# The first layer's start: modulation in pairs applied tile by tile, eight projections abreast, five modulation tiles later

## What is computed

```python
cond = silu(c)
for l in range(2):
    sh_a, sc_a, gt_a, sh_f, sc_f, gt_f = (cond @ w_ada[l] + b_ada[l]).reshape(6, 1024)
    u = rms_norm(x, g_mix[l]) * (1 + sc_a) + sh_a
    proj = u @ w_in[l]            # fox q,k,v | fox_f | mla_q | mla_kv | mla_kr | sb q,k,v | gate
    ...                           # three attentions, each gated, merged
    x = x + gt_a * (merged @ w_out[l])
    u = rms_norm(x, g_ffn[l]) * (1 + sc_f) + sh_f
    x = x + gt_f * ((silu(u @ w_gate[l]) * (u @ w_up[l])) @ w_down[l])
```

## Time and profile before

| | us |
|---|---|
| median of 3 runs | 2159.16 |
| lowest, highest | 2157.09, 2160.19 |
| profiled execution | 2153.36 |
| its span | 2151.4 |

### The profile page before, as it was taken

The page is one execution under the profiler, slowest core; times in us unless marked ns, Lnnn a source line. Parts: engine busy times, 40 slices in busy tenths (PEclk is TensorE's granted clock), DMA queues, the critical chain, the costliest instruction groups (busy, mean ns, idle before and its releaser), DMA issues.

```text
span 2151.4 us, 36731 instructions
## 1 busy us (share of the span) xinstructions
PE 2060.7 (96%) x13888; PEld 1853.3 (86%) x13888; DVE 1620.5 (75%) x2661; ACT 1159.7 (54%) x2053; POOL 127.1 (6%) x202
## 2 busy tenths in 40 slices
PE   4999999999999999998997999999999999999998
PEld 3988989999988989998875778888877888999997
DVE  7688878966788878968777788787888436757983
ACT  3547756645556756646637355353444235656872
POOL 2100000000000000004000000001100000000000
PEclk9999999999999999999999999999999999999999
DMA  7875556765766546865440424546563222244553
GB/s 298 283 242 195 189 167 214 268 204 169 264 234 207 177 166 219 289 207 196 157 166 11 167 88 147 190 133 214 194 208 113 93 98 92 95 137 138 193 189 109
DMA packets 106896, 383.03 MB, mean 178 GB/s; under 512 B 11632, under 2 KB 16368, under 8 KB 105456
## 3 DMA queue, kind: packets, MB, share of 16 engines
q1 hardware_dynamic: 78304, 282.23, 38.4%
q0 software_dynamic: 25344, 92.29, 12.7%
q10 hardware_dynamic: 3088, 6.29, 0.8%
HBM read 379.71 MB, written 1.05 MB: 177 GB/s over the span
## 4 chain that ended last, share of the span: by engine, by line
PE 86%; DVE 8%; ACT 3%; DMA 1%; issue 1%; DVEq 0%; SPq 0%; ACTq 0%
PE ps L1021 21%; PE ps L1025 21%; PE ps L1024 21%; PE ps L1040 3%; PE ps L1044 3%; PE ps L1045 3%; PE ps L1061 2%; PE ps L1065 2%; PE ps L1064 2%; DVE ring_l L2133 2%; DVE ada_junk L2158 2%; PE ps L1500 1%; ACT ring_r L1550 1%; DMA ring<-tape_in 1%; PE ps L1256 1%
## 5 line engine op out<-in xcount | busy, mean ns | idle before, releaser
L1021 PE MATMUL ps<-part,ring_l 128*128 128x256 f32 (+1 forms) x3456 | 1049.7, 304 | 11.9 <-DVE ring_l L2133 7.2
L1025 PE MATMUL ps<-part,ring_r 128*128 128x256 f32 (+1 forms) x3456 | 1041.7, 301 | 0.0
L1024 PE MATMUL ps<-part,ring_r 128*128 128x256 f32 (+1 forms) x3456 | 1038.2, 300 | 0.0
L1550 ACT ACTIVATE ring_r<-ring 128x1024 fp32r<-128x1024 f32 x511 | 530.7, 1057 | 414.5 <-DMA ring<-tape_in 303.5
L2133 DVE TENSOR_TENSOR ring_l<-ring,ring_r 128x1024 fp32r<-128x1024 f32 x511 | 620.2, 1227 | 156.0 <-ACT ring_r L1550 153.5
L1021 PEld LDWEIGHTS ps<-part,ring_l 128*128 128x128 f32 x3456 | 651.8, 189 | 44.5 <-issue 6.8
L1024 PEld LDWEIGHTS ps<-part,ring_r 128*128 128x128 f32 x3456 | 651.6, 189 | 27.4
L1025 PEld LDWEIGHTS ps<-part,ring_r 128*128 128x128 f32 x3456 | 650.4, 188 | 26.7
L2158 DVE SCALAR_TENSOR_TENSOR ada_junk<-work 128x1024 bf16<-128x1024 f32 x272 | 339.6, 1248 | 47.7 <-DMA work<-adas_in 35.5
L1061 PE MATMUL ps<-part,ring_l 128*128 128x256 f32 (+1 forms) x328 | 107.3, 327 | 7.0 <-DVE part L2133 3.8
L1065 PE MATMUL ps<-part,ring_r 128*128 128x256 f32 (+1 forms) x328 | 105.3, 321 | 0.0
(11 more groups left out here) (251 smaller groups left out, 2094.4 us busy)
## 6 DMA issues: line engine op xcount, KB each, us to landing
ring<-tape_in SPq DMA_DIRECT2D x514, 512.0 KB, 3.4
work<-adas_in POOLq DMA_DIRECT2D x176, 512.0 KB, 4.6
work<-ada_first_in SPq DMA_DIRECT2D x8, 1024.0 KB, 13.2
work<-bias_in ACTq DMA_DIRECT2D x1, 2048.0 KB, 8.1
x<-x_t_in SPq DMA_DIRECT2D x1, 1024.0 KB, 15.7
work<-cond_in SPq DMA_DIRECT2D x1, 1024.0 KB, 18.2
x<-ctx_in ACTq DMA_DIRECT2D x1, 1024.0 KB, 7.4
x<-dist_in ACTq DMA_DIRECT2D x1, 1024.0 KB, 6.8
```

The lines of the kernel that those rows point to most:

```text
L1021: mm = pe.matmul(dst, lhsT=wl, rhs=mr, start=(k == 0), stop=False)
L1024: pe.matmul(dst, lhsT=wr, rhs=mr, start=False, stop=False)
L1025: mm = pe.matmul(dst, lhsT=wr, rhs=ml, start=False, stop=(k == len(moving) - 1))
L1550: act.activation(ring_r[:, q % RING, :], ring[:, q % RING, :], ACT.Copy).then_inc(rounded, 1)
```

## The change

The start of layer 0 is written anew, and some work is moved.

- **SP** loads `x`, constants and parameters first, then alternately a pair of modulation tiles (scale k, shift k; 1 MB) and a panel. POOL, not SP, issues the rest of the constants, the positions, the other two condition vectors, `par2` and `misc`.
- **POOL** no longer rounds or splits panels 0 to 2. ACT and DVE do.
- **DVE** makes the first pair of products, scales all eight tiles of `x` by the inverse root, and then goes k by k: a product, the rest of the u tile before, a product, a panel's split. Lines 2294 and 2300 no longer run in layer 0's first norm.
- **ACT** makes gain k and shift k by two 128x1 activations, and applies them to tile k twice (once whole into `first_u`, once rounded).
- **PE** runs 6 pairs ahead, and all eight `fox_qk` of layer 0 abreast, so that panel k holds the tiles of feature k. Layer 1 keeps three.
- The sigmoid of the other two condition vectors goes from one place on ACT (three instructions over 128x2048) into six over 128x1024 beside `sb_qk`; its product on DVE (128x2048) goes behind `sb_v`. Both in layer 0 only.
- The five products beside `fox_qk` leave in both layers; all later ones keep their places, and the last five (ADA_TAIL) come after the 16 early ones, in feed-forward steps 16 to 20. They are gates of the second residual, needed from `down3` on.

```diff
-ADA_FIRST_PARTS = 8
+ADA_TAIL = 5
...
-REST_FIRST, REST_NORM, REST_ENTRY = 22, 6, 13
+REST_FIRST, REST_NORM = 6, 6
...
-ADA_BEFORE = {"fox_qk": 5, "lat": 4, "sb_qk": 5, "q_rope": 2}
+ADA_BEFORE = {"lat": 4, "sb_qk": 5, "q_rope": 2}
 ADA_IN_STEP = (2, 2, 2, 1, 2, 1, 1, 1, 1, 1, 1, 1)
 ABREAST = 3
+QK_ABREAST = (KD, ABREAST)
...
+            early = min(max(t - ADA_HEAD + 1, 0), ADA_EARLY)
+            return t + early
+
+        def ada_target(t):
+
+            if t < ADA_HEAD:
+                return ADA_EARLY + t
+            return t - ADA_HEAD if t < ADA_HEAD + ADA_EARLY else t
...
-            for q in range(ADA_FIRST_PARTS):
-                if q < FIRST:
-                    sp.dma_start(ring[:, q, :], tape[q]).then_inc(landed[q], 16)
-                some = slice(q * ADA_EARLY // ADA_FIRST_PARTS, (q + 1) * ADA_EARLY // ADA_FIRST_PARTS)
-                sp.dma_start(ada_first[:, some, :], ada_first_in[:, some, :]).then_inc(loaded[f"ada{q}"], 16)
-                if q == FIRST - 1:
-                    sp.dma_start(xt, x_in).then_inc(loaded["x"], 16)
-                if q == FIRST:
-                    sp.dma_start(cst[:, 0:SUM_CONSTS], consts[:, 0:SUM_CONSTS]).then_inc(loaded["sums"], 16)
+            sp.dma_start(xt, x_in).then_inc(loaded["x"], 16)
+            sp.dma_start(cst[:, 0:SUM_CONSTS], consts[:, 0:SUM_CONSTS]).then_inc(loaded["sums"], 16)
             sp.dma_start(par1_all[:, :, :], par1).then_inc(loaded["par1"], 16)
-            for s in range(FIRST, RING):
-                sp.dma_start(ring[:, s, :], tape[s]).then_inc(landed[s], 16)
-            sp.dma_start(cst[:, SUM_CONSTS:], consts[:, SUM_CONSTS:]).then_inc(loaded["cst"], 16)
-            sp.dma_start(cond[:, 1:N_COND, :].rearrange("p a n -> p (a n)"), cond_in[D:N_COND * D].partition_broadcast(P))\
-                .then_inc(loaded["cond"], 16)
-            sp.dma_start(rope_0[:, 0, :].bitcast(I32), pos_in.partition_broadcast(P)).then_inc(loaded["pos"], 16)
-            sp.dma_start(par2[:, :, :], par2_in).then_inc(loaded["par2"], 16)
-            sp.dma_start(misc[:, :], misc_in).then_inc(loaded["misc"], 16)
+            for k in range(KD):
+                sp.dma_start(ada_first[:, 2 * k:2 * k + 2, :], ada_first_in[:, 2 * k:2 * k + 2, :]).then_inc(loaded[f"ada{k}"], 16)
+                if k < RING:
+                    sp.dma_start(ring[:, k, :], tape[k]).then_inc(landed[k], 16)
...
-            for s in range(FIRST):
-
-                pool.wait_ge(landed[s], 16)
-                pool.tensor_copy(ring_r[:, s, :], ring[:, s, :]).then_inc(rounded_first, 1)
-                pool.wait_ge(rounded_first, s + 1)
-                pool.tensor_tensor(ring_l[:, s, :], ring[:, s, :], ring_r[:, s, :].bitcast(F32), ALU.subtract).then_inc(parted, 1)
-
-            pool.wait_ge(*done("fox_qk0", 0))
+            pool.wait_ge(*ada_early(ADA_EARLY - 3))
+            pool.dma_start(cst[:, SUM_CONSTS:], consts[:, SUM_CONSTS:]).then_inc(loaded["cst"], 16)
+            pool.dma_start(rope_0[:, 0, :].bitcast(I32), pos_in.partition_broadcast(P)).then_inc(loaded["pos"], 16)
+            pool.wait_ge(*ada_early(ADA_EARLY - 1))
...
+                    if l == 0 and t == 2 * ADA_SLOTS - 1:
+                        pool.dma_start(cond[:, 1:N_COND, :].rearrange("p a n -> p (a n)"), cond_in[D:N_COND * D].partition_broadcast(P))\
+                            .then_inc(loaded["cond"], 16)
+                        pool.dma_start(par2[:, :, :], par2_in).then_inc(loaded["par2"], 16)
+                        pool.dma_start(misc[:, :], misc_in).then_inc(loaded["misc"], 16)
...
-                project_abreast([f"fox_qk{f}" for f in range(ABREAST)], uk, lambda k: u_made(k, l))
-                for f in range(ABREAST, 2 * WT):
+                project_abreast([f"fox_qk{f}" for f in range(QK_ABREAST[l])], uk, lambda k: u_made(k, l))
+                for f in range(QK_ABREAST[l], 2 * WT):
...
-                shifted(0, 0, RING if l else None)
-                round_panels(RING)
-
-
+                    for k in range(KD):
+                        round_panels(k + 1)
+                        act.wait_ge(*mod_made(1, l))
+                        act.wait_ge(*ada_early(2 * k + 1))
+                        act.activation(gs_mix[:, k:k + 1], ada_sums[:, KD + k, 0:1], ACT.Identity, bias=gs_ffn[:, k:k + 1],
+                                       scale=par_of("g_mix")[:, k:k + 1]).then_inc(mod_first.sem, 1)
+                        act.activation(mod[:, k, 0:1], ada_sums[:, k, 0:1], ACT.Identity, bias=par_of("b_ada")[:, k:k + 1])\
+                            .then_inc(mod_first.sem, 1)
+                        act.wait_ge(*scaled(k, l))
+                        act.wait_ge(*mod_first(2 * k + 1))
+                        for dst in (first_u[:, k, :], u_r[:, k, :]):
+                            a = act.activation(dst, sq[:, k, :], ACT.Identity, bias=mod[:, k, 0:1], scale=gs_mix[:, k:k + 1])
+                        a.then_inc(u_round.sem, 1)
+                    round_panels(KD + 2)
+                else:
+                    shifted(0, 0, RING)
+                    round_panels(RING)
+
+
+                queries_keys("fox", fox_qk)
                 if l == 0:
-                    act.wait_ge(loaded["cond"], 16)
-                    sigmoid(cond_e[:, 1:N_COND, :], cond[:, 1:N_COND, :], prep_act, 1)
                     act.wait_ge(*prep(10))
-                    act.activation(rope_s[:, :], rope_0[:, 0, :], ACT.Sin).then_inc(prep_act.sem, 1)
-                    act.activation(rope_c[:, :], rope_0[:, 1, :], ACT.Sin).then_inc(prep_act.sem, 1)
+                    act.activation(rope_s[:, :], rope_0[:, 0, :], ACT.Sin).then_inc(mod_first.sem, 1)
+                    act.activation(rope_c[:, :], rope_0[:, 1, :], ACT.Sin).then_inc(mod_first.sem, 1)
...
-                queries_keys("sb", sb_qk, lambda f: round_latent(f - 1) if f else None)
+                def beside_sb(f):
+
+                    if f:
+                        round_latent(f - 1)
+                    if l == 0 and f == 1:
+                        act.wait_ge(loaded["cond"], 16)
+                    if l == 0 and 1 <= f <= 6:
+                        n, step = 1 + (f - 1) // 3, (f - 1) % 3
+                        dst, src = cond_e[:, n, :], cond[:, n, :]
+                        if step > 0:
+                            act.wait_ge(*prep_act(3 * n + step - 1))
+                        if step == 1:
+                            act.activation(dst, dst, ACT.Ln, bias=1.0).then_inc(prep_act.sem, 1)
+                        else:
+                            act.activation(dst, src if step == 0 else dst, ACT.Exp, scale=-1.0).then_inc(prep_act.sem, 1)
+
+                queries_keys("sb", sb_qk, beside_sb)
...
-            for t in range(ADA_EARLY):
-                ada_product(ada_first[:, t, :], ada_sums[:, t, 0:1], cond[:, 0, :], ada_early,
-                            ada_early(t - 1) if t else None, (loaded[f"ada{t * ADA_FIRST_PARTS // ADA_EARLY}"], 16))
+            dve.wait_ge(loaded["par1"], 16)
+            dve.tensor_copy(par[:, :], par1_all[:, 0, :]).then_inc(mod_made.sem, 1)
+            dve.wait_ge(*mod_made(0))
+            dve.scalar_tensor_tensor(gs_ffn[:, :], par_of("b_ada")[:, KD:2 * KD], 1.0, par_of("g_mix"), ALU.add, ALU.mult)\
+                .then_inc(mod_made.sem, 2)
+
+            def first_product(t):
+
+                to = KD + t // 2 if t % 2 == 0 else t // 2
+                ada_product(ada_first[:, t, :], ada_sums[:, to, 0:1], cond[:, 0, :], ada_early,
+                            ada_early(t - 1) if t else None, (loaded[f"ada{t // 2}"], 16))
+
+            def first_rest(k):
+
+                dve.wait_ge(*u_round(k))
+                rest(u_l[:, k, :], first_u[:, k, :], u_r[:, k, :]).then_inc(u_made.sem, 1)
+
+            first_product(0)
+            first_product(1)
             dve.wait_ge(loaded["x"], 16)
-            dve.memset(ada_sums[:, :, 1:2], 0.0).then_inc(x_ready.sem, KD)
-            dve.wait_ge(loaded["par1"], 16)
-            dve.wait_ge(*ada_early(ADA_EARLY - 1))
+            dve.wait_ge(*rstd_made(0))
+            for k in range(KD):
+                dve.tensor_tensor(sq[:, k, :], xt[:, k, :], rstds[0], ALU.mult).then_inc(scaled.sem, 1)
+            for k in range(KD):
+                if k >= 1:
+                    first_product(2 * k)
+                    first_rest(k - 1)
+                    first_product(2 * k + 1)
+                split_panels(k + 1)
+            first_rest(KD - 1)
...
-                    first_modulation(0)
-                dve.wait_ge(*rstd_made(0, l))
-                normalised(0, gs_mix, 0)
-
-
-                ahead("fox_qk0", l)
-                if l == 0:
-                    rope_angles()
+                if l > 0:
+                    dve.wait_ge(*rstd_made(0, l))
+                    normalised(0, gs_mix, 0)
+                    ahead("fox_qk0", l)
                 def adas_beside(n, name=None):
                     for i in range(n):
```

(20 more changed lines are left out.)

51 lines of the change are left out of this document (26 added, 25 removed).

## The result

The changed kernel took 2135.19 us in the median of four executions (2132.52 to 2140.49), the kernel before 2158.80 in the median of four beside it. The ratio is 0.9896, with a 95% interval of 0.9878 to 0.9915: faster by 1.0%, 23.6 us, where 18.4 were forecast. The time lies 1.3 us under the low end of the range (2136.5). In six more executions the same kernel took 2138.53 in the median (0.9906, 0.9886 to 0.9926), inside the range. All ten together have a mean of 2137.4 (median 2137.5), and the kernel before, in 58 executions beside the experiments, one of 2157.7 (median 2158.0). That is 20.2 us between the means, with a 95% uncertainty of some 2.4, from standard deviations of 3.4 and 3.7 us. Two executions of this study, one of the kernel before (4111 us) and one of a variant (3461 us), ran in a slow state and are left out of every number here.

The account below looks back on a forecast made before the run. It took the start as bound by DVE's products, with PE doing about 49 us of nothing useful; -20.2 there and +1.8 behind sb_v gave -18.4, from the median of 2159.2 to 2141 us, range 2136.5 to 2148 (8 in 10).

Parts of the forecast that it names:

- the range: Whole kernel: the time was to lie between 2136.5 and 2148 us, eight times in ten.
- The start, steps 1 to 7: Layer 0 from the condition load to fox_v's end: fox_v ends at 62.6 instead of 82.8, gaining 20.2 us.
- Step 5: Loop of the start: DVE paces at 3.78 us a round; ACT needs 2.7, PE 2.79, and transfers land ahead.
- PE's clock, 0: First projections of layer 0: the first group or two may run at half clock, PE catches up by the fourth; cost 0.
- The product behind sb_v, 1.8: DVE behind sb_v: the 2.29 us condition product delays the first pv by 1.8 us, bounds 0 and 2.3.
- The products that leave fox_qk and those that come late, 0 and 0: fox_qk and feed-forward: leaving is worth 0 more; late products cost 0 in both layers, 5.8 us each without cover.
- The sum, -18.4: Whole kernel: 20.2 us gained at the start less 1.8 lost behind sb_v.
- the median 2 either way: Whole kernel: bound of 2 us either way for the median, one of the forecast's terms.
- the product at 0: Behind sb_v: lower bound of the condition product's cost, 0 if ACT's part of the chain came last, not DVE's.
- DVE's start: Start of layer 0: bound of 1.5 us either way on DVE's start.
- the span of its terms: Whole kernel: forecast with the bounds of its terms, 2137 to 2145 us, given a chance of 0.75.

Follow-up runs that it names:

- unread22: Changed kernel with 22 unread pairs ahead of the first projection instead of 6; 2138.96 us (4 executions), 0.9916 of the kernel before.
- pair_ahead: Changed kernel with the second pair of products made ahead of the wait for the inverse root, not in the loop; 2135.78 us (4 executions), 0.9912.
- abreast3: Changed kernel with three projections abreast in the first layer instead of eight; 2153.94 us (10 executions), 0.9978 of the kernel before.
- tail0: Changed kernel without late products: five back beside fox_qk in layer 2, five more in layer 1's attention steps; 2142.16 us (4 executions), 0.9933.
- the repeated profile: Profile of the changed kernel run again with no edit; 2138.53 us (6 executions), 0.9906 of the kernel before.
- the kernel with all three moves: Changed kernel with condition product ahead of sb_v's copies, second pair of products ahead of the root, rests of u on POOL; 2135.58 us (6 executions), 0.9908.

## Why the prediction was right or wrong

**The start, steps 1 to 7.** Right to about half a microsecond. DVE's multiply of the condition came at 8.84 and not 9.71 (the load had landed 0.9 earlier), but as forecast it was the root that set the scaling, at 16.84 against 16.9. The loop's pitch was 3.76 against 3.78, its seventh turn at 43.24 against 43.5, the last rest began at 47.83 and ended at 48.25 against 48.3, PE's last group began at 48.31, fox_v was copied at 62.03 against 62.6. The gain there is 20.8 in the recorded profile against 20.2. In the five other profiles with the same start it is 20.6 to 22.0, since the root comes between 15.7 and 17.1. Step 5, that DVE and not transfers, ACT or PE sets the pace, was shown from both sides: 22 unread pairs (unread22) changed PE and nothing moved, the second pair ahead of the root (pair_ahead) took 2.3 us from DVE and 2.3 went. One reading is off: the 86 matmuls of the window 50 to 60 include two that reach over its ends, and from one to the next it is 0.120 there, not 0.1163. It does little harm, since fox_v's 11.5 was taken as what 192 of them leave of the rest up to 82.83.

**PE's clock, 0.** Right, by unread22. The first group ran at half the clock, as said, and PE had caught up by the fifth tile (the text said the fourth). What the text did not see is how near the other side lay: three abreast (abreast3) has the clock at 0.50 through the whole loop, at waits of 1.2 to 1.5 us. That eight abreast kept its clock was argued from one row at 4 us of idle time and one at 1, neither of which has pauses of that kind; in part it was luck.

**The product behind sb_v, 1.8.** Near in size, 1.5, and wrong about where. PE waits 1.54 at the keys, and the 0.29 at the first pv, which was there before, stays or goes. Moving the product gave back 1.06, doubling it cost 2.3, so the chain has no cover, as argued.

**The products that leave fox_qk and those that come late, 0 and 0.** Right within the 0.1 and 0.8 us by which the distance moved in the kernel without late products (tail0).

**The sum, -18.4.** The means differ by 20.2, the repeated profile from that of before by 18.7 ahead of the last stage. Of the 1.8 between forecast and means about 1 is the start, which in the mean of six profiles gained 21.3 and not 20.2, and 0.3 the wait at the keys. The rest is within the uncertainty of 2.4.

**The step that failed is the range**, in its term "the median 2 either way", and in how its low end was added up. By the text's own bounds the low side is 1.8 (the product at 0), 1.5 (DVE's start) and 2 (the median) under 2140.8, which is 2135.5; the text has 2137 for the span of its terms and 2136.5 for the range, though its high end, 2145, is the plain sum. The recorded 2135.2 lies under all three, 0.3 under the lowest. The 2 for the median has no source in the text beyond three executions of before that agreed within 3.1 us. Over 58 executions they spread from 2148.9 to 2165.7, with a standard deviation of 3.7; the median of four then strays by about 2.3 (1.25 x 3.7 / 2), and the median of three from which the forecast starts by 2.7 (1.25 x 3.7 / 1.73), together 3.5. Eight times in ten that stays within 1.28 x 3.5 = 4.5; with the 1.5 for DVE's start beside it the low end would have been 2134.8. (This is worked out afterwards, from executions that the text did not have.) The forecast of 2140.8 was high by 3.4 against the mean of 2137.4: 1.5 of it because the median that it started from lay that much above 2157.7, 1.8 from the sum. The recorded median of 2135.2 lies 2.2 under the mean, which is one such error, of chance; the median of six more executions, 2138.5, would have been inside the range, and that too would have been chance. No mechanism of the change is seen behind it: the traces show no place, beyond the start, at which it gains a microsecond.

## What to carry to other kernels

Where an engine paces a start, count its instructions, one after another, and put the end where the last needed one leaves it: the result is good to half a microsecond, and the other engines' troubles, a halved clock among them, fall into their slack. Ask of each burst of matmuls not only whether PE keeps up but whether its pauses leave it its clock: the same loop with three projections abreast, and waits of 1.2 to 1.5 us, kept PE at 1.2 GHz, with eight it did not. Work made piece by piece pays only where something can use the pieces: the new loop without eight abreast was worth 0.65 us. And take the spread of a kernel's times from many executions before a range is set to a fraction of a per cent; three that agree say little.

## What the runs showed that was not expected

- **A wait of 1 to 1.6 us can be followed by half the clock, or not.** Behind the same 1.54 us of idle time the window read 0.66 in one execution and 1.00 in another; behind the same 1.39 and 0.93 it read 0.54 in the changed kernel and 1.00 in the kernel before. Each stretch costs up to 1.7 us, and the fourteen profiled executions have three to ten of them behind the start.
- **PE has two paces in the last stage, at the same granted clock.** 179 or 172 matmuls of 256 columns in 20 us, 0.113 or 0.118 us from one to the next in the rows, over some 120 us. The pace is there from the first matmul of the projections after the last unread pairs. No edit here was seen to choose it.
- **POOL's small passes cost DVE their own time.** Beside a subtraction of 128 x 256 that takes POOL 0.93, DVE's second product of the turn took 0.35 longer, as much as DVE would have spent on doing it. The passes themselves are uneven: POOL's first took 3.05 us here, its later ones mostly 0.93, and in the kernel with all three moves the first three took 5.12, 1.71 and 1.46 us. DVE works without a pause beside the long ones; whether POOL waits for it there was not tested:

```profile
18.96 3.05 POOL L954 TENSOR_TENSOR part<-work,part 128x256 fp32r<-128x256 f32 x1 [18.50 <-ACT part L1632]
```
